# Third pieces of three-part transposes on TensorE: 128 columns wide instead of 64, in a two-layer streaming encoder step

## The reference

```
z = x @ w_in            # columns: SWA q|k|v, FoX q|k|v, forget logits, gate_a, gate_b
branch A: grouped-query attention (8 q heads, 2 kv heads, 64 wide), rotary, sinks, chunk mask
branch B: forgetting attention (8 heads, 64 wide), logits += F[t] - F[s]
y = (sigmoid(gate_a) * (o_a @ w_pa) + sigmoid(gate_b) * (o_b @ w_pb)) @ w_o
x = LayerNorm(alpha * x + y)
f = (gelu(causal_dwconv3(x @ w_gate)) * (x @ w_up)) @ w_down
x = LayerNorm(alpha * x + f)
```

## Time and profile before

| | |
|---|---|
| time, median of 3 runs | 981.52 us (981.27 to 981.65) |
| profiled execution, span from first to last instruction | 979.4 us |
| TensorE products / weight loads | 953.2 us (97%) / 902.9 us (92%) |
| VectorE / ScalarE / GpSimd | 603.3 us (62%) / 509.4 us (52%) / 20.0 us (2%) |
| mean granted TensorE clock | 0.986 of full |
| DMA | 133.18 MB, mean 136 GB/s |

### The profile page before, as it was taken

How to read it: one execution, slowest core, us unless ns; L and a number is a source line. 1 busy time by engine, 2 the same in 40 slices (tenths; PEclk the granted TensorE clock), 3 DMA queues, 4 the chain that set the end, 5 groups by cost and what they waited for, 6 DMA issues and landing times.

```text
span 979.4 us, 18915 instructions
## 1 busy us (share of the span) xinstructions
PE 953.2 (97%) x6526; PEld 902.9 (92%) x6526; DVE 603.3 (62%) x1210; ACT 509.4 (52%) x979; POOL 20.0 (2%) x35
## 2 busy tenths in 40 slices
PE   6999999999999999999889999999999999999996
PEld 5988889999899999999789888899989999999993
DVE  3765545477876656546576665447787656564544
ACT  3863544434855555533377545444467555553323
POOL 1000000000000000000000000000000000000000
PEclk9999999999999999999989999999999999999996
DMA  9744433454365454544733453435527454545411
GB/s 255 187 118 125 130 93 108 132 155 127 117 176 164 135 166 131 161 141 141 179 89 101 116 141 97 117 108 151 152 65 215 140 158 144 155 136 161 146 52 54
DMA packets 257794, 133.18 MB, mean 136 GB/s; under 512 B 22391, under 2 KB 254875, under 8 KB 257563
## 3 DMA queue, kind: packets, MB, share of 16 engines
q1 hardware_dynamic: 256058, 126.95, 46.3%
q0 software_dynamic: 1632, 4.93, 1.4%
HBM read 127.42 MB, written 4.57 MB: 135 GB/s over the span
## 4 chain that ended last, share of the span: by engine, by line
PE 94%; DVE 3%; ACT 1%; issue 1%; DMA 1%; SPq 0%; DVEq 0%; ACTq 0%
PE bank L619 27%; PE bank L621 27%; PE bank L620 27%; PE bank L689 3%; PE bank L841 2%; PE bank L690 2%; DVE roped_b L1399 1%; PE bank L808 1%; PE bank L635 1%; PE bank L638 1%; PE bank L795 1%; PE bank L792 1%; PE bank L641 1%; PE bank L803 1%; DMA gates<-in_x_sample 1%
## 5 line engine op out<-in xcount | busy, mean ns | idle before, releaser
L619 PE MATMUL bank<-act_hi,w_hi 128*128 128x320 f32 x1312 | 412.8, 315 | 3.0 <-DVE w_lo L1166 2.8
L620 PE MATMUL bank<-act_lo,w_hi 128*128 128x320 f32 x1312 | 406.6, 310 | 0.0
L621 PE MATMUL bank<-act_hi,w_lo 128*128 128x320 f32 x1312 | 406.6, 310 | 0.0
L1166 DVE TENSOR_TENSOR w_lo<-raw,w_hi 128x1024 fp32r<-128x1024 f32 (+1 forms) x236 | 283.5, 1203 | 111.1 <-ACT w_hi L909 110.2
L909 ACT CAST w_hi<-raw 128x1024 fp32r<-128x1024 f32 (+1 forms) x236 | 244.2, 1035 | 142.2 <-PE bank L621 136.2
L619 PEld LDWEIGHTS bank<-act_hi,w_hi 128*128 128x128 f32 x1312 | 247.6, 189 | 10.1 <-issue 5.7
L620 PEld LDWEIGHTS bank<-act_lo,w_hi 128*128 128x128 f32 x1312 | 247.7, 189 | 0.2
L621 PEld LDWEIGHTS bank<-act_hi,w_lo 128*128 128x128 f32 x1312 | 247.5, 189 | 0.0
L619 PE MATMUL bank<-h_hi,w_hi 128*128 128x320 f32 x352 | 109.4, 311 | 0.0
L621 PE MATMUL bank<-h_hi,w_lo 128*128 128x320 f32 x352 | 108.8, 309 | 0.0
L620 PE MATMUL bank<-h_lo,w_hi 128*128 128x320 f32 x352 | 108.8, 309 | 0.0
(11 more groups left out here) (201 smaller groups left out, 1011.4 us busy)
## 6 DMA issues: line engine op xcount, KB each, us to landing
raw<-in_w_in SPq DMA_DIRECT2D x62, 512.0 KB, 3.9
raw<-in_w_gate SPq DMA_DIRECT2D x44, 512.0 KB, 3.9
raw<-in_w_up SPq DMA_DIRECT2D x44, 512.0 KB, 4.7
raw<-in_w_down SPq DMA_DIRECT2D x32, 448.0 KB, 3.5
raw<-in_w_o SPq DMA_DIRECT2D x16, 512.0 KB, 3.7
raw<-in_w_down SPq DMA_DIRECT2D x16, 512.0 KB, 3.7
raw<-in_w_in SPq DMA_DIRECT2D x16, 256.0 KB, 4.4
raw<-in_w_pa SPq DMA_DIRECT2D x32, 128.0 KB, 2.8
```

What stands on the lines that cost most here:

```text
L619: pe.matmul(out, wh, hi[:, k0 + c, :], start=begin and c == 0, stop=False)
L620: pe.matmul(out, wh, lo[:, k0 + c, :], start=False, stop=False)
L621: mm = pe.matmul(out, wl, hi[:, k0 + c, :], start=False, stop=end and c == n_chunks - 1)
L1166: ve.tensor_tensor(w_lo[:, slot, :, :].rearrange("p c e -> p (c e)")[:, 0:w], raw[:, slot, 0:w], hi.bitcast(F32), ALU.subtract).then_inc(l ...
```

## The change

Where a 64-column piece was turned, 128 columns are now read, so that the piece too is a transpose of full width; the 64 rows more that this writes to PSUM are not read. For keys the further columns are the cache's, for probabilities the next block, for x the next tile's first 64 frames; `stage` gets 64 further columns, and `xT` 64 behind its last tile, both set to zero once by VectorE. At the end, the third piece of tile k is done once tile k + 1 is ready, since it reads it; the last two third pieces stand together at the end. The third pieces of the forget logits, the convolution rows and the inputs are as before.

```diff
-        xT = sb("xT", [P, KC, TOK])
+        x_flat = sb("xT", [P, KC * TOK + TS])
+        xT = x_flat[:, 0:KC * TOK].rearrange("p (k t) -> p k t", t=TOK)
...
-        stage = sb("stage", [P, 2, TOK])
+        stage = sb("stage", [P, 2, TP + P])
...
                     for t in range(3):
-                        w = P if t < 2 else TS
-                        mm = turned(b[0:w, t * P:(t + 1) * P], src[:, t * P:t * P + w])
+                        mm = turned(b[:, t * P:(t + 1) * P], src[:, t * P:(t + 1) * P])
                     done(mm)
...
                     turned(b[:, 0:P], pr[:, 6 * P + TS:6 * P + TS + PAST])
-                    done(turned(b[0:TS, P:2 * P], pr[:, 6 * P:6 * P + TS]))
+                    done(turned(b[:, P:2 * P], pr[:, 6 * P:7 * P]))
...
             for o in range(KC):
                 pe.wait_ge(y_ready, o + 1)
-                for t in range(3):
-                    w, c = P if t < 2 else TS, o % (KC // 2)
-                    mm = turned(Y_BANKS[3 * (o // (KC // 2)) + t][0:w, c * P:(c + 1) * P], xT[:, o, t * P:t * P + w])
+                half, c = o // (KC // 2), o % (KC // 2)
+                for t in range(2):
+                    mm = turned(Y_BANKS[3 * half + t][:, c * P:(c + 1) * P], xT[:, o, t * P:(t + 1) * P])
+                    if c == KC // 2 - 1:
+                        mm.then_inc(y_turned, 1)
+
+
+                for k in (o - 1, o) if o == KC - 1 else (o - 1,) if o > 0 else ():
+                    half, c = k // (KC // 2), k % (KC // 2)
+                    mm = turned(Y_BANKS[3 * half + 2][:, c * P:(c + 1) * P],
+                                x_flat[:, k * TOK + TP:k * TOK + TP + P])
                     if c == KC // 2 - 1:
                         mm.then_inc(y_turned, 1)
...
-            act.wait_ge(set_once, 5)
+            act.wait_ge(set_once, 7)
...
             ve.memset(a_ext[:, :, 0:2], 0.0).then_inc(set_once, 1)
+            ve.memset(stage[:, :, TOK:TP + P], 0.0).then_inc(set_once, 1)
+            ve.memset(x_flat[:, KC * TOK:KC * TOK + TS], 0.0).then_inc(set_once, 1)
```

More of the change, by code:

```diff
@@ L314, in build @@
         conv = sb("conv", [P, 2, EXT - 2])
-        hf = stage
+        hf = stage[:, :, 0:TOK]
         tails = sb("tails", [P, 4 * FT])
@@ L942, in after @@
                         swap(l, 0, b, 1.0)
-                    sc.copy(stage[:, k, :], b[:, 0:TOK]).then_inc(copied, 1)
+                    sc.copy(stage[:, k, 0:TOK], b[:, 0:TOK]).then_inc(copied, 1)
                 elif kind in ("ga", "gb"):
@@ L1329, in step @@
                 elif kind == "rope":
-                    x = stage[:, 0, :] if i == 0 else qT[:, i - 1, :]
+                    x = stage[:, 0, 0:TOK] if i == 0 else qT[:, i - 1, :]
                     out = kT[:, 0, 0:TOK] if i == 0 else qT[:, i - 1, :]
```

## The result

The changed kernel takes 968.09 us (967.06 to 970.82, 4 runs), the kernel before beside it 981.39 us (981.03 to 981.65, 4 runs): 13.3 us less. The ratio as recorded is 0.9879, with a 95% interval of 0.9857 to 0.9901 (that of the two medians is 0.9864), so it is faster by 1.2 to 1.4%. The forecast was 973.3 us with a range of 967.5 to 977. So the sign and the range were right, and the size was 5.2 us short.

A forecast was written before the change was run, and what follows sets the result against it. The prediction took TensorE as the bound: 9.7 us gained at values tiles and turns, plus 3.1 at the end, minus 4.6 for clock falls, is 8.2 us off the median 981.5, giving 973.3 us, range 967.5 to 977.

The forecast's parts named there:

- TensorE is the limit, and time off it counts in full: Whole kernel: TensorE is busy 97% of the span, so time saved between units counts unless the next instruction waits elsewhere.
- Rival 2: Transposes followed by a unit's product: the slack stays, 16 places lose 0.19 us each, 976.3 us; chance 0.13.
- The switch of the stationary operand to 64 columns and back does: At the 64-column pieces: this switch causes the slack; dropping it gains 0.45 us before a unit's product.
- The key tiles give nothing: Key tiles in both layers: faster turning gains no time, since VectorE and ScalarE set TensorE's restart.
- I take 2.3 us between the two, in both layers: Behind the key tiles: more idle time makes the clock fall, costing 2.3 us in each layer.
- The term of 4.6 us: Loss from clock falls behind the key tiles of both layers together: 4.6 us, bounds nothing and 6.0.
- rival 1: Key tiles: the clock stays up in one or both layers; one fall 971.0 us, none 968.7; chance 0.27.
- the places: Values tiles and turns of probabilities: full-width transposes gain 4.85 us a layer, 9.7 us for both.
- Rival 4: Waits for weights, as at 503.5 us, grow by at most 2 us a layer: 975 to 977 us; chance 0.08.
- The end: End of the program, eight tiles of x: ScalarE sets TensorE's pace and the last store comes earlier, gaining 3.1 us.
- Rival 3: Attention stages: the clock falls there too, each fall costing 1.7 us or more, so the kernel is slower; chance 0.04.

The follow-up runs named there:

- Experiments 1: The changed kernel with its 44 third pieces as products with the identity again, now 128 columns wide: 970.75 us, ratio 0.9908.
- Experiment 2: The kernel before with its 64-column pieces turned by a 64-column transpose instead of a product: 968.74 us, ratio 0.9880.
- experiments 5: The changed kernel with the five key tiles as before, by products of 64 columns: 964.84 us, ratio 0.9847.
- experiment 6: The changed kernel timed again, 968.15 us, and the changed kernel with identity transposes filling the idle time at the key tiles, 965.13 us.
- Experiment 4: The kernel before with only the change at the end of the program (the eight tiles of x and the memset): 977.43 us, ratio 0.9969.
- the last kernel of experiment 8: The changed kernel with identity transposes filling the key tiles' idle time and products of zeros ahead of the first inputs: 963.88 us, ratio 0.9824.

## Why the prediction was right, and where it was short

- **TensorE is the limit, and time off it counts in full: right.** From the first transpose of each place to the second product of the next unit, the timelines of before and after give for layer one: 8 places in front of a unit's product 8 x 0.45, values tile 8 0.40 (0.85 with turn 2 behind it), values tiles 6 and 9 in front of scores 0.25 each, values tile 7 0.10, all as priced; only the first turn gave 0.07 in place of 0.25. That is 4.68 us a layer, forecast 4.85, and layer two gives the same. Rival 2 (slack stays) is out by the row at 39.22. The first key tile stands 4.93 us earlier, a little more than its 4.68, since the clock rose sooner at the start: products of 320 columns take 0.31 us in place of 0.47 from 20.0 us on, before from 20.8 on.
- **"The switch of the stationary operand to 64 columns and back does" bring the slack: wrong as put.** The convolution rows told a product with 88 columns from one with 64, and I took this for a statement on all instructions. Experiments 1 and 2 show that neither the width nor the product alone has a price beyond the product's second pass; the pair has. The price was right because the changed kernel drops both at once, so in this point the number owes something to luck. Experiment 2 shows what this means: the extra columns, the padding behind `xT` and the delayed third pieces at the end weren't needed for the gain.
- **The key tiles give nothing: right.** It is 5.02 us from the first key tile to the restart, before and in every later kernel; in the changed one with idle time of 1.25 and 1.75 us, forecast 1.35 and 1.95.
- **"I take 2.3 us between the two, in both layers" was the step that failed.** Idle time at the key tiles can bring the clock down, as forecast, and experiments 5 and 6 show it by taking the idle time away. But in both profiles of the changed kernel it did so in one layer of two (in experiments 1 and 2 in both), and a fall cost 1.4 us in every layer that had one, not 2.3. The price was taken from stages at the start of layer two and behind 503.5 us, the second of which was 6.8 us long; behind the key tiles the clock was low for 3.4 us. The term of 4.6 us was 1.4 in the profile. This is rival 1 ("one fall: 971.0").
- **A term that I had not listed: the old stages at half clock.** At the start of layer two and behind the wait at 503.5 us the clock was low for 3.4 and 6.8 us before, and 3.4 and 3.4 in the changed kernel; the wait itself was 2.75 and is 1.76 us. Between the first product of layer two and the last sums the kernel gained 10.37 - 5.22 = 5.15 us although a fall of 1.4 us had been added, so 1.9 us more than the 4.68 of the places. I ascribe it to these two, and it fits their size: in the profile of the change once more (experiment 6) the stage at 501.2 isn't there at all, and from the first product of layer two to its first key tile it takes 222.40 us in place of 224.05, so 1.65 less for one stage of 3.4 us (230.61 before the change). It was not tested by itself, and it differs between executions of one kernel, so it is no sure gain of the change. Rival 4 (weight supply takes the gain back) went the other way.
- **The end: 2.6 us, forecast 3.1.** TensorE, ScalarE, the copies and SyncE moved as written: the last store is issued 2.84 us earlier. The stores then took 3.0 us to the end of the span in place of 2.8.
- **Rival 3 (falls in the attention stages): did not occur.** Runs of up to 11 transposes there stayed at 1.00.
- **Sum:** 9.7 + 3.1 - 4.6 = 8.2 us was forecast. The profiles show 9.4 for the places (two times 4.68), 2.6 for the end, 1.4 lost to a fall, and 2.4 left over, of which 1.9 lies in layer two between its first product and its last sums: 13.0. That the result lies in the range, 0.6 us over its lower end, is in part luck: the fall that stayed away and the term that wasn't listed moved it the same way.

What stays open is why the clock falls in one layer or run and not in another with the same idle time. Experiment 4 had a fall in layer one with 1.35 us of idle time, which the kernel before passed twice without one.

## What to carry to other kernels

Look at the distance between the starts of TensorE's instructions where their shapes change: a single 64-column float32 product among full-width work cost 0.45 us more than the transpose's 0.11, and its own record showed nearly none of that. Work that is hidden behind a wait may still be worth keeping or replacing, because idle TensorE time can cost the clock of the stage behind it: here each such fall cost 1.4 us, and the kernel with ten hidden pieces made slower was the faster one. Before widening a piece to full width, try the same piece in the other mode; it may be all that the gain needs.

## What the runs showed of the hardware that was not expected

- A float32 transpose of 64 columns passes among full-width work without slack (0.47 us for the place), and so does a product of 128 columns (0.59, its second pass included); a product of 64 columns does not (0.92). A second narrow product behind the first adds 0.23 us, its two passes.
- Transposes can keep the clock up and raise it. Filled with nothing but transposes for 5 us, the stretch at the key tiles stayed at 1.00 in all four layers that had the fill (experiment 6 and the last kernel of experiment 8). In the changed kernel the clock was 0.51 while 24 transposes of x ran almost without gaps from 955.47 on, and 0.99 from 962.0. It isn't so in every execution: in experiment 6 the same 24 transposes ran for the same 6.58 us from 952.55 on, and the clock was 0.50 from 949.6 to the end.
- The Trainium skill, page "TensorE: Matmul & The Clock Gate", Part 4, on which the prediction drew, says that full clock doesn't engage for transposes. The 0.99 at 962.0 and the filled key tiles at 1.00 contradict that. Whether transposes count for less than products do, as it also says, these runs leave open.
- The same program has executions with different falls of the clock. The ten runs of experiment 4 lie in groups near 975 and 978.5 us, with mean granted clocks of 0.994 and 0.989.
